# Expert weights in transfers of 2 MB, routing chunk by chunk, and one gather per expert

## The reference

```
mixed = concat(rms_norm(attn, norm_attn_out), rms_norm(ssm, norm_ssm_out))
h  = h + mixed @ w_out
hn = rms_norm(h, norm_ffn)
logits = hn @ w_router + b_router              # 32 experts
top_v, top_i = top_k(logits, 4);  top_w = softmax(top_v)
for each of the 32 experts:
    hdn = hn @ w_up + b_up                     # 1024 x 2048
    gt, up = min(hdn[:, :1024], 7), clip(hdn[:, 1024:], -7, 7)
    act = (up + 1) * gt * sigmoid(1.702 * gt)
    acc += gate * (act @ w_down + b_down)      # 1024 x 1024
h = h + acc
h = h + sigmoid(rms_norm(h, norm_ple) @ w_ple_gate) * (p @ w_ple_proj)
y = rms_norm(h)                                # with the final norm's weights
```

## Time and profile before

| | |
|---|---|
| median of three runs | 1316.38 us |
| the profiled execution's own time | 1311.35 us |
| its span, first to last instruction | 1309.6 us |
| TensorE busy | 1174.1 us (90%) |
| VectorE, ScalarE, GpSimd busy | 353.8, 171.9, 95.4 us |
| moved by the transfers | 438.56 MB, 335 GB/s over the span |
| mean granted TensorE clock | 0.97 |

### The profile page before, as it was taken

One profiled execution on the slowest core, in us unless ns is written; L12 is line 12 of the kernel. 1 busy time (PEld: TensorE's weight loads), 2 busy tenths in 40 slices (PEclk: granted clock), 3 DMA queues, 4 the chain that ended last, 5 costly groups with the idle time before them and its releaser, 6 DMA issues.

```text
span 1309.6 us, 14918 instructions
## 1 busy us (share of the span) xinstructions
PE 1174.1 (90%) x5551; PEld 546.2 (42%) x5551; DVE 353.8 (27%) x693; ACT 171.9 (13%) x330; POOL 95.4 (7%) x211
## 2 busy tenths in 40 slices
PE   3997888999999999999899998999998999999875
PEld 2754566533433343334334333433343343334264
DVE  6799823212111111121211111111212111111133
ACT  2113322110011001010100100100011001100022
POOL 4674400000000000000000000000000000000000
PEclk9997889998999999999999999999999999997988
DMA  8413033299999999999999999999999999999600
GB/s 298 148 40 158 11 131 129 79 418 418 417 394 417 418 416 417 417 417 419 418 418 417 419 418 418 417 417 417 417 418 419 417 419 416 419 416 417 279 1 34
DMA packets 89189, 438.56 MB, mean 335 GB/s; under 512 B 13632, under 2 KB 16832, under 8 KB 55344
## 3 DMA queue, kind: packets, MB, share of 16 engines
q1 hardware_dynamic: 88528, 437.60, 82.2%
q10 hardware_dynamic: 624, 0.45, 0.1%
HBM read 436.65 MB, written 2.41 MB: 335 GB/s over the span
## 4 chain that ended last, share of the span: by engine, by line
PE 64%; DMA 12%; DVE 10%; SPq 7%; ACT 4%; issue 3%; ACTq 0%; DVEq 0%
PE ps L926 24%; PE ps L943 14%; DMA ring_up<-in_w_up_dram 11%; PE ps L910 7%; SPq L397 4%; SPq L404 3%; PE ps L804 2%; PE ps L1065 2%; PE ps L518 2%; PE ps L921 2%; PE ps L933 1%; ACT region L1258 1%; PE ps L598 1%; PE ps L869 1%; DVE region L1720 1%
## 5 line engine op out<-in xcount | busy, mean ns | idle before, releaser
L926 PE MATMUL ps<-ring_up,region 128*64 128x512 f32 x2112 | 463.5, 594 | 5.5 <-DMA ring_up<-in_w_up_dram 5.4
L926 PEld LDWEIGHTS ps<-ring_up,region 128*64 128x64 f32 x2112 | 147.3, 137 | 319.4 <-issue 296.9
L943 PE MATMUL ps<-ring_dn,region 128*64 128x512 f32 x1056 | 242.1, 612 | 22.7 <-ACT region L1258 22.7
L1716 DVE TENSOR_SCALAR region<-ps 128x512 f32<-128x512 f32 x33 | 22.8, 692 | 718.4 <-PE ps L926 718.4
L943 PEld LDWEIGHTS ps<-ring_dn,region 128*64 128x64 f32 x1056 | 74.7, 140 | 169.1 <-issue 138.3
L910 PE MATMUL ps<-region,n_tok 128*128 128x256 f32 (+1 forms) x384 | 95.8, 394 | 0.0
L1256 ACT ACTIVATE region<-region 128x512 f32<-128x512 f32 x33 | 20.8, 631 | 497.8 <-DVE region L1716 497.8
L869 PE MATMUL ps<-region 128*128 128x264 f32 (+1 forms) x272 | 69.4, 399 | 15.0 <-DVE fb L1711 12.4
L485 POOL COPY region<-kst 128x64 f32 (+1 forms) x33 | 7.9, 239 | 1020.5 <-PE ps L926 956.0
L910 PEld LDWEIGHTS ps<-region,n_tok 128*128 128x128 f32 (+1 forms) x384 | 67.3, 188 | 31.2 <-issue 24.2
L1268 ACT ACTIVATE region<-ps 64x512 f32<-64x512 f32 x66 | 39.1, 592 | 245.8 <-PE ps L943 245.4
(11 more groups left out here) (347 smaller groups left out, 823.5 us busy)
## 6 DMA issues: line engine op xcount, KB each, us to landing
ring_up<-in_w_up_dram SPq DMA_DIRECT2D x264, 1024.0 KB, 19.1
ring_dn<-in_w_down_dram SPq DMA_DIRECT2D x132, 1024.0 KB, 17.9
ring_up<-in_w_in_dram SPq DMA_DIRECT2D x4, 1280.0 KB, 10.5
ring_dn<-in_w_out_dram SPq DMA_DIRECT2D x1, 4096.0 KB, 25.4
ring_up<-in_w_ple_gate_dram SPq DMA_DIRECT2D x4, 1024.0 KB, 11.5
x_tok<-in_x_prompt_dram SPq DMA_DIRECT2D x2, 512.0 KB
ring_up<-in_w_glu_dram SPq DMA_DIRECT2D x1, 1024.0 KB, 15.3
region<-in_w_ple_proj_dram SPq DMA_DIRECT2D x1, 1024.0 KB
```

What stands on the lines that cost most here:

```text
L926: m = mm(ps[64 * (q % 2):64 * (q % 2) + 64, HID_B + q // 2, :], xe[:, k, slots], ring_up[:, k, q * 512:(q + 1) * 512], start=False, stop=( ...
L943: m = mm(ps[64 * half:64 * half + 64, OUT_B, :], act_t[:, f % 4, 64 * (f // 4):64 * (f // 4) + 64], ring_dn[:, f, 512 * half:512 * half + ...
```

## The change

**SP.** The up weights come in 4 transfers of 2 MB: for each partition two rows of 8 KB that lie 128 rows (1 MB) apart. The down weights come in 2 transfers of 2 MB: for each partition four neighbouring rows, 16 KB in one run. A transfer waits until both its 1 MB places (down: both pairs of rows) are released. Because a partition now holds rows 4p to 4p + 3 of the down weights, the activation's columns are transposed with a step of four (`act_cols`).

**Loop.** `pair` replaces `quad`. `gather(t)` picks the tokens of one expert: the selection (64 columns) is stationary, the rows (512 columns) move, two halves of the array side by side; ACT copies the result (`xr`), `turn_gathered` transposes it in four steps, and DVE scales it into `xe`. The gather of the next expert and one part of `combine` stand between `up` and `turn_activations`; the next expert's bias products and `turn_gathered` stand between `turn_activations` and `down`; another part of `combine` stands behind `down`.

**Ahead of the loop.** The output projection is done by chunks of tokens (128, 128, 8), with tokens as output rows, and by halves (attention, state-space). The norms' weights are multiplied into `w_out` (ACT, earlier) and `router` (DVE). The state-space norm becomes a factor in the residual add. Each chunk is transposed before its norm's root is known, and the root is multiplied into its logits (`choose`). Chunk 0 is routed while chunk 1 is projected.

The diff, cut to its core:

```diff
-            up_w = A["w_up"][0].rearrange("e (k p) n -> e k p n", p=P)
-            dn_w = A["w_down"][0].rearrange("e (s k p) n -> e s p k n", p=P, k=2)
+            up_w = A["w_up"][0].rearrange("e (k j p) n -> e k p j n", p=P, j=2)
+            dn_w = A["w_down"][0].rearrange("e (s p k) n -> e s p k n", p=P, k=4)
             def expert(e, t, first=False):
-                for k in range(UP):
+                for k in range(UP // 2):
...
-                        sp.wait_ge(Z["up_free"], t * UP + (k + 1 - UP))
-                    sp.dma_start(ring_up[:, k], up_w[bass.ds(e, 1), k].rearrange("e p n -> (e p) n")
+                        sp.wait_ge(Z["up_free"], t * UP + (2 * k + 2 - UP))
+                    sp.dma_start(ring_up[:, 2 * k:2 * k + 2], up_w[bass.ds(e, 1), k].rearrange("e p j n -> (e p) j n")
                                  ).then_inc(up_in[k], 16)
-                for s in range(DN):
+                for s in range(DN // 2):
                     if first:
-                        sp.wait_ge(Z["mix_ps"], KD)
+                        sp.wait_ge(Z["mix_ps"], (7, 9)[s])
                     else:
-                        sp.wait_ge(Z["dn_free"], t * DN + (s + 1 - DN))
-                    sp.dma_start(ring_dn[:, 2 * s:2 * s + 2], dn_w[bass.ds(e, 1), s].rearrange("e p k n -> (e p) k n")
+                        sp.wait_ge(Z["dn_free"], t * DN + (2 * s + 2 - DN))
+                    sp.dma_start(ring_dn[:, 4 * s:4 * s + 4], dn_w[bass.ds(e, 1), s].rearrange("e p k n -> (e p) k n")
                                  ).then_inc(dn_in[s], 16)
...
+            def mixed(c, k0, b0):
+                for half in range(2):
+                    for k in range(k0, k0 + 4):
+                        m = mm(bank(b0 + half), fb[:, k, c * P:(c + 1) * P], w_out[:, k, half * 512:half * 512 + 512],
+                               start=(k == k0), stop=(k == k0 + 3))
+                    m.then_inc(Z["mix_ps"], 1)
+                    yield half
...
+            def route(c, ks):
+                t0, nt = CHUNKS[c]
+                for k in ks:
+                    m = mm(ps[0:nt, (4, 5, 7)[c], 0:NE], fb[:, k, t0:t0 + nt], router[:, k, :], start=(k == 0),
+                           stop=(k == KD - 1))
...
+            def gather(t, a):
+                pe.wait_ge(Z["sel_rdy"], t + 1)
+                if not isinstance(t, int) or t > 0:
+                    pe.wait_ge(Z["xg_sb"], t)
+                for c, (t0, nt) in enumerate(CHUNKS):
+                    for half in range(2):
+                        m = mm(ps[64 * half:64 * half + 64, XG_B, :], sel[0:nt, c, a],
+                               n_tok[0:nt, c, 512 * half:512 * half + 512], start=(c == 0), stop=(c == 2))
+                m.then_inc(Z["xg_ps"], 1)
+            def turn_gathered(t):
+                pe.wait_ge(Z["xg_sb"], t + 1)
+                if not isinstance(t, int) or t > 0:
+                    pe.wait_ge(Z["xe_rdy"], t)
+                for i in range(4):
+                    m = tr(ps[:, XT_B, i * P:(i + 1) * P], xr_cols[:, i // 2, i % 2], ident)
+                m.then_inc(Z["xt_ps"], 1)
...
                 for j in range(4):
-                    m = tr(ps[:, TURN_B, j * P:(j + 1) * P], act_v[:, j * P:(j + 1) * P], ident)
+                    m = tr(ps[:, TURN_B, j * P:(j + 1) * P], act_cols[:, j], ident)
...
-            def quad(q, place=None):
...
+            def pair(p, a, place=None):
+                t = 2 * p
+                up(t)
+                gather(t + 1, 1)
+                if place == "first":
+                    embedding(range(4, 6))
+                else:
+                    combine_pair(p - 1, 1 - a, (0,))
+                turn_activations(t)
+                bias(t + 1)
+                turn_gathered(t + 1)
+                down(t)
+                if place == "first":
+                    embedding(range(6, KD))
+                else:
+                    combine_pair(p - 1, 1 - a, (1,))
+                turn_selection(p)
+                up(t + 1)
+                gather(t + 2, 0)
...
+                turn_activations(t + 1)
...
+                    bias(t + 2)
+                turn_gathered(t + 2)
...
+                down(t + 1)
...
@@ scalar
+            def scale_w_out(ks):
+                for k in ks:
+                    f(w_out[:, k], w_out[:, k], ACT.Copy, scale=vecs[:, V_OUT + k:V_OUT + k + 1]
+                      ).then_inc(Z["w_out_g"], 1)
...
+            def gathered(t):
+                act.wait_ge(Z["xg_ps"], t + 1)
+                f(xr, bank(XG_B), ACT.Copy).then_inc(Z["xg_sb"], 1)
...
@@ vector
+            def choose(c, n_):
...
+                chain(V.scalar_tensor_tensor(logits[r, c], ps[r, (4, 5, 7)[c], 0:NE], stat[r, c, 2:3], router_b[r],
+                                             ALU.mult, ALU.add))
+                chain(V.max(top[r, c, 0:8], logits[r, c]))
...
```

More of the change, by code:

```diff
@@ L854, in _ @@
-            m.then_inc(Z["cnt_ps"], 1)
-            for c, (t0, nt) in enumerate(CHUNKS):
-                m = tr(ps[0:NE, 3, t0:t0 + nt], gate[0:nt, c, 0:NE], ident[0:nt, 0:nt])
-            m.then_inc(Z["gtr_ps"], 1)
-            embedding(range(6, KD))
-            def combine(n_, weights, outputs, parts=range(4), rows_=slice(0, P)):
+            list(mixed(0, 0, ATT_O))
+            pe.wait_ge(ld_p, 48)
+            pe.wait_ge(Z["glu_sig"], KM)
+            for k in range(2):
+                for c, (t0, nt) in enumerate(CHUNKS):
+                    m = tr(ps[:, 2 + k, t0:t0 + nt], p_tok[0:nt, c, k * P:(k + 1) * P], ident[0:nt, 0:nt])
@@ new lines, in _ @@
+            pe.wait_ge(Z["pT_sb"], 1)
+            pe.wait_ge(Z["s_ot"], 1)
+            pe.wait_ge(Z["ssm_n"], 1)
+            for half in range(2):
+                for k0 in (0, 4):
+                    for j in range(4):
+                        m = mm(ps[32 * j:32 * j + 32, NB_O + half, :], fb[:, k0 + j, T - W_ROWS:T],
+                               w_out[:, k0 + j, half * 512:half * 512 + 512], start=(k0 == 0), stop=(k0 == 4))
+            m.then_inc(Z["mix_ps"], 1)
+            pe.wait_ge(Z["back_add"], 3)
@@ new lines, in _ @@
+            turned(0, (0,))
+            pe.wait_ge(Z["back_add"], 4)
+            pe.wait_ge(Z["ssm_root"], 1)
+            turned(0, (1,))
+            for half in mixed(1, 0, ATT_O):
+                if half == 0:
+                    pe.wait_ge(Z["norm_sb"], 6 + 2)
+                    route(0, range(KD))
+                    pe.wait_ge(Z["raw_sb"], 1)
+                    for h in range(2):
+                        m = mm(ps[0:NB, NB_O + h, :], kst[:, K_NTH + W_ROWS - NB:K_NTH + W_ROWS], s_raw[:, h],
+                               start=True, stop=True)
+                    m.then_inc(Z["back_ps"], 1)
@@ new lines, in _ @@
+            for half in range(2):
+                for k in range(4, KD):
+                    if (half, k) == (1, 4):
+                        pe.wait_ge(Z["back_add"], 7)
+                        turned(2, range(2))
+                    if (half, k) == (1, 7):
+                        pe.wait_ge(Z["back_add"], 8)
+                        turned(1, (0,))
+                    m = mm(bank(SSM_O + half), fb[:, k, P:2 * P], w_out[:, k, half * 512:half * 512 + 512],
+                           start=(k == 4), stop=(k == KD - 1))
+                m.then_inc(Z["mix_ps"], 1)
@@ L864, in combine @@
+            count_masks(1, (0, 2))
+            for c, (t0, nt) in enumerate(CHUNKS):
+                m = mm(ps[:, 4, 3 * NE:4 * NE], ones[0:nt, :], mask[0:nt, c, :], start=(c == 0), stop=(c == 2))
+            m.then_inc(Z["cnt_ps"], 1)
+            embedding(range(2, 3))
+            def combine(n_, weights, outputs, parts=range(4), rows_=slice(0, P), last=False):
                 for j in parts:
-                    if not isinstance(n_, int) or 4 * n_ + j > 1:
-                        pe.wait_ge(Z["cmb_read"], 4 * n_ + j - 1)
+                    if not isinstance(n_, int) or 4 * n_ + j > 0:
+                        pe.wait_ge(Z["cmb_read"], 4 * n_ + j - (1 if last and j > 0 else 0))
@@ L1020, in visit @@
                 pe.wait_ge(Z["gt_sb"], PAIRS + 1 + v)
-                combine(PAIRS + 1 + v, g_t[:, 0], pair_outputs(0), rows_=slice(0, C))
-            gather(0)
+                combine(PAIRS + 1 + v, g_t[:, 0], pair_outputs(0), rows_=slice(0, C), last=True)
+            pe.wait_ge(Z["norm_scaled"], 6)
+            gather(0, 0)
+            embedding(range(3, 4))
+            turn_gathered(0)
+            pe.wait_ge(ld_bup, 32)
+            bias(0)
+            pe.wait_ge(Z["mask_sb"], 4)
+            pe.wait_ge(Z["pp_sb"], 2)
+            for c, (t0, nt) in enumerate(CHUNKS):
+                m = tr(ps[0:NE, OUT_B, t0:t0 + nt], gate[0:nt, c, 0:NE], ident[0:nt, 0:nt])
+            m.then_inc(Z["gtr_ps"], 1)
             quad(0, "first")
@@ L1196, in _ @@
                 att_root(b)
+                if b == 0:
+                    scale_w_out(range(4, KD))
             cache_copies()
@@ new lines, in _ @@
```

(12 more changed lines are left out.)

680 lines of the change are left out of this document (351 added, 329 removed).

## The result

| | before | after |
|---|---|---|
| median | 1316.50 us (4 runs, 1314.91 to 1318.67) | 1277.43 us (4 runs, 1273.65 to 1282.41) |
| profiled execution, its span | 1311.35, 1309.6 us | 1274.09, 1272.3 us |
| moved, over the span | 335 GB/s | 345 GB/s |
| mean granted TensorE clock | 0.970 | 0.977 |

The ratio is 0.9704, with a 95% interval of 0.966 to 0.9749: 2.5 to 3.4% faster. The forecast was 1279 us.

A forecast was written before the change was run, and what follows sets the result against it. Transfers were taken to bound the loop, nearly balanced with PE. Packets -13.3, start -14.8 (queue and two-place wait included), PE 0 and tail -9.2 sum to -37.3: 1316.4 becomes 1279 us, by itself 1267 to 1291, overall range 1258 to 1302.

The forecast's parts named there:

- Packet length: Expert loop: down weights in 16 KB runs save 0.43 us per expert, period 29.71 us; -13.3 us over 31 periods.
- PE within a period: Mid-loop: PE's work falls from 29.4 to 28.3 us per expert, worth nothing because the transfers set 29.71; 0 us.
- Start: Ahead of the loop: first up product at 235.0, 17.5 us earlier; waiting for two places takes back 1.74 us.
- The queue dry in the first pairs: First two pairs of experts: queue runs dry now and then, 3 us against about 2 before; +1.0 us.
- Tail: Behind the last weights: the visit's down ends 20.3 us after its last up piece, before 29.5; -9.2 us.
- the strided loads: Expert loop: step-of-four activation loads, if four times as long, add 1.74 us per expert; rival 1291 us, chance 0.15.
- PE as the bound: Expert loop: the same rival; PE needs 30.0 to 30.1 us per expert against 29.71, +12 us, 1291 us, chance 0.15.
- the others: Whole kernel: 16 KB runs buy nothing (1292 us, 0.10); all better bounds (1267, 0.08); stream loses rate (1325, 0.07).

The follow-up runs named there:

- the other: The changed kernel, unaltered, profiled in a further set of six runs: median 1281.45 us, ratio 0.9737 to the kernel before; its traced span is 1280.8 us.
- all ten runs: The changed kernel, unaltered: four runs with median 1277.43 us and a further six with median 1281.45 us.

## Why the prediction came out right

By its own steps, on the three cuts:

- **Packet length (-13.3): right in mechanism and size, incomplete in its condition.** 0.613 us forecast, 0.612 measured; period 29.71 forecast, 29.67 measured; undone, 11 to 13 us. The line it used had two points, 4 and 8 KB, through which any line goes; that 16 KB lies on it too was a step beyond the rows, and it held. But it was told as a term by itself, and the next step as 0.
- **PE within a period (0): the number is right for the sum, the reading wrong.** 28.3 us forecast, 28.24 measured, wait for weights 1.3. Yet with the old order the same transfers gave no gain (1.0021; without the step 0.9939). The order of PE is what lets the longer packets count; the reason "the transfers set 29.71" was true only because of the step that was priced at nothing.
- **Start (-15.8 with the wait for two places): the mechanism is right, the size depends on the clock in the head.** First up product 235.0 forecast; 228.8 in the profiled run and 237.2 in the other. From the product that the earlier trace rows have at 171.03 to that one the sum had 64.0 us; the two executions took 60.2 (from 168.63) and 64.9 (from 172.28), so that "until 171.0" holds for neither. The head gave -22.0 in the profiled pair. The -13.6 of the other sets a long head against the profiled execution of before, which lies 5 us under its kernel's median.
- **The queue dry in the first pairs (+1.0): the step that was mis-sized.** Instead of 3 us the hole costs 6.4 in the rows above, beside dips like that at 252 to 256 (328 GB/s). In the first 100 us of the stream, after and then before:

```profile
233.65:333.65 100.00, 99.78 (x452) 37.66 (x450) 16.61 (x31) 11.35 (x21) 0.71 (x3) 0.95 0.95 388
255.65:355.65 100.00, 94.63 (x432) 35.99 (x429) 17.21 (x26) 8.65 (x15) 0.95 (x4) 0.97 1.01 415
```

Against 424 the change lost 8.5 us there; before lost 0.5 against 417 and 1.7 in the next 100 (410 GB/s). The term is +6.3 or so instead of +1.0. Of its causes only the extra products and the wait for half of `down` were named; the lower clock and the longer way from `up` to `down` were not. Moving the products removed the hole, changing the piece's size did not.
- **Tail (-9.2): right for the change, mis-sized for the kernel before.** The visit's `down` ended at 1205.4 (1196.66 + 8.78), 20.0 us behind its last up piece, which left SP at 1159.7 and landed 25.8 us later, at 1185.5; the forecast was 20.3. But in the kernel before that piece left at 1189.7 and took 26.6 us, the longest of the last twelve transfers into `ring_up`:

```profile
DMA to landing us min/median/max: 10.2/18.9/26.6
```

So it landed at 1216.3 and not at 1213.0, a time worked out from a mean rate; `down` ended 26.2 us behind it, not 29.5. The tail gave -6.2.

For the loop's cut the forecast was -13.3 + 1.0 and some 8.3 of the tail's 9.2 (the gate leaves 4.5 us behind the visit's last up piece before, 3.8 ahead of it in the forecast): -20.6. Measured: -15.1. Of the 5.5 missing the early loss explains about 5 and the tail 2.0 (the gate left 1.2 behind that piece before and 5.1 ahead of it after); the period gave about 1.3 back (30.14 to 29.67, over 31 periods), and the three close to within 1 us. In the profiled pair the head's surplus of 6.2 made up for it, to the microsecond: that is luck. The median of all ten runs, 1280.6, is within 2 us of the forecast, and 35.9 under the median before; if loops and ends are as in the traces, the heads differ by some 20.6 there, and a surplus of nearly 5 us covers the loop again. This is an estimate, since the kernel before has one trace.

Of the rivals, the strided loads were real (62 ns each) but had cover; PE as the bound came true only with the old order; the others did not occur. One small misreading changes nothing: the plateau of the earlier trace rows is 416 to 419 GB/s, not 417 to 419.

## What to carry to other kernels

Where two engines are nearly balanced, a gain on the one is worth only the slack of the other, so price the edits that make slack together with the one that uses it. A few narrow products on the path where a ring is first refilled can cost more than their time: put them where PE waits anyway, but count that slack, since two of 1.15 us in an expert with 1.3 us of slack were already too many. Longer runs in memory gain where transfers bind, up to 16 KB per packet here. When totals scatter by half a per cent, cut the execution at queue events that all versions share, and compare the pieces.

## What the runs showed of the hardware

- With 16 queues busy, a packet into SBUF costs 0.160, 0.311 and 0.612 us at 4, 8 and 16 KB: 0.009 us and 0.151 for each 4 KB, with nothing lost at 16 KB.
- In these transposes the load of the 128x128 float32 stationary operand takes 141 to 145 ns from neighbouring numbers, 203 to 208 with a step of two or four. For other products these figures don't hold: the gate product's loads (L1132) take 190 ns from neighbouring numbers.
- The granted clock fell to 0.50 right behind products over 32 rows, one after another, and not in the version that has them apart (1.00 from 280 to 350); that these products are the cause is not shown. With the old order and the new transfers it also fell in one of four experts, behind waits of 0.96 and 0.69 us. In the head it falls for different stretches from run to run: 8.5 us between two executions of one program.
